# A two-block transformer layer on one core: padded parameter rows, the last expert behind the overflow tests, a final stage by halves, and down weights in 16 KB runs with a strided moving operand

## The reference

```python
(jax.nn.silu(xblk @ w1[e]) * (xblk @ w3[e])) @ w2[e]     # w1, w3: 1024 x 512, w2: 512 x 1024
```

## Time and profile before

| | |
|---|---|
| median of three runs (lowest, highest) | 1033.22 us (1032.62, 1033.77) |
| the profiled execution's own time | 1032.23 us |
| its span | 1030.4 us, 16914 instructions |
| PE busy (matmuls) | 96% of the span |
| PE weight loads busy | 74% |
| DVE, ACT, POOL busy | 38%, 37%, 12% |
| mean granted clock of TensorE | 0.988 of full |
| moved by DMA | 308 MB, 299 GB/s over the span |

### The profile page before, as it was taken

How to read it: one execution, slowest core, us unless ns; L and a number is a source line. 1 busy time by engine, 2 the same in 40 slices (tenths; PEclk the granted TensorE clock), 3 DMA queues, 4 the chain that set the end, 5 groups by cost and what they waited for, 6 DMA issues and landing times.

```text
span 1030.4 us, 16914 instructions
## 1 busy us (share of the span) xinstructions
PE 988.3 (96%) x7393; PEld 767.3 (74%) x7393; DVE 392.5 (38%) x750; ACT 377.1 (37%) x612; POOL 121.8 (12%) x81
## 2 busy tenths in 40 slices
PE   7999999999999999979999999989999999999996
PEld 6888789976555555545555555558989999999995
DVE  4446456853222111121222111127335444774475
ACT  4545646641111111111111111226445555554443
POOL 2110021020000000000000000002321111441122
PEclk8999999999999999998999999999999999999999
DMA  8974295788999999999999999997545544445301
GB/s 271 365 273 177 96 346 217 300 315 348 424 426 425 423 425 426 426 420 426 424 425 423 427 425 424 424 401 283 184 163 187 187 171 164 164 167 204 141 1 42
DMA packets 74829, 308.07 MB, mean 299 GB/s; under 512 B 5585, under 2 KB 12146, under 8 KB 58362
## 3 DMA queue, kind: packets, MB, share of 16 engines
q1 hardware_dynamic: 70962, 302.16, 74.0%
q10 hardware_dynamic: 3784, 4.73, 1.4%
HBM read 305.82 MB, written 2.63 MB: 299 GB/s over the span
## 4 chain that ended last, share of the span: by engine, by line
PE 85%; DVE 7%; ACT 4%; issue 2%; POOL 1%; DMA 1%; SPq 0%; ACTq 0%; DVEq 0%
PE bank L782 82%; DVE arena L1306 3%; DVE arena L1303 2%; PE bank L1251 1%; ACT arena L2058 1%; DVE wR L1300 1%; DMA arena<-in_rows 1%; PE bank L993 1%; DVE arena L1300 1%; ACT wR L1881 1%; POOL wR L2256 1%; ACT arena L2088 0%; DVE hTR L1300 0%; ACT arena L2086 0%; ACT arena L2111 0%
## 5 line engine op out<-in xcount | busy, mean ns | idle before, releaser
L782 PE MATMUL bank<-hTR,wR 128*128 128x256 f32 x2520 | 313.8, 284 | 4.2 <-DVE wR L1300 1.2
L782 PEld LDWEIGHTS bank<-hTR,wR 128*128 128x128 f32 x2520 | 305.1, 192 | 8.2 <-issue 4.2
L782 PE MATMUL bank<-ring,arena 128*64 128x256 f32 (+3 forms) x1680 | 229.6, 439 | 7.1 <-issue 7.1
L1300 DVE TENSOR_TENSOR wR<-ring,wR 128x1024 fp32r<-128x1024 f32 x126 | 157.8, 1259 | 133.2 <-ACT wR L1881 132.6
L1881 ACT ACTIVATE wR<-ring 128x1024 fp32r<-128x1024 f32 x161 | 168.5, 1055 | 109.2 <-PE bank L782 107.4
L782 PEld LDWEIGHTS bank<-ring,arena 128*64 128x64 f32 (+2 forms) x1680 | 115.3, 137 | 103.1 <-issue 59.7
L782 PE MATMUL bank<-arena 128*64 128x256 f32 (+7 forms) x1178 | 166.5, 406 | 0.7 <-DVE small L1432 0.7
L1306 DVE SCALAR_TENSOR_TENSOR arena<-bank,small,arena 128x256 f32<-128x256 f32 x32 | 15.5, 484 | 346.9 <-ACT arena L2058 346.9
L2029 ACT ACTIVATE arena<-bank,small 64x512 f32<-64x512 f32 x62 | 42.4, 684 | 280.5 <-PE bank L782 280.1
L782 PEld LDWEIGHTS bank<-arena 128*64 128x64 f32 (+3 forms) x1178 | 92.3, 144 | 62.4 <-issue 28.3
L2256 POOL TENSOR_TENSOR wR<-ring,wR 128x1024 fp32r<-128x1024 f32 x35 | 85.5, 2443 | 321.7 <-ACT wR L1881 321.7
(11 more groups left out here) (209 smaller groups left out, 823.2 us busy)
## 6 DMA issues: line engine op xcount, KB each, us to landing
ring<-in_w SPq DMA_DIRECT2D x39, 2048.0 KB, 21.5
ring<-in_w_in SPq DMA_DIRECT2D x29, 2048.0 KB, 8.4
arena<-in_w SPq DMA_DIRECT2D x25, 2048.0 KB, 19.0
ring<-in_w SPq DMA_DIRECT2D x42, 1024.0 KB, 19.4
arena<-in_w SPq DMA_DIRECT2D x22, 1024.0 KB, 20.9
ring<-in_w_ada SPq DMA_DIRECT2D x6, 2048.0 KB, 7.9
ring<-in_w_o SPq DMA_DIRECT2D x2, 2048.0 KB, 12.4
ring<-in_w_o_attn SPq DMA_DIRECT2D x2, 2048.0 KB, 7.9
```

The lines of the kernel that those rows point to most:

```text
L782: return pe.e.matmul(o, l, r, start=start, stop=stop)
L1300: return eng.tensor_tensor(o, a, b, op)
```

## The change

It does nine things.

1. The rows table is padded on the host with zeros from 113 to 128 rows, and all 128 are loaded.
2. The identity's DMA moves from SP's queue, where it was the first, to ACT's, ahead of ACT's first wait.
3. PE runs three warm-up matmuls behind the rows' transpose instead of five.
4. The transposes `turn1` and `turn3` get PSUM banks 2 to 5, one each, instead of banks 0, 1, 6 and 0 again.
5. A down weight is loaded by one DMA of 2 MB with four rows, 16 KB, a partition.
6. So that the hidden columns fit these rows, half `h` of an up product takes of every four columns of its weights the two from 2 `h` on. The moving operand becomes 128 pairs with a gap of two elements behind each.
7. ACT and DVE make the overflow test ahead of the last expert, which stands whole in both branches.
8. The gating of `wx0` stands between the splits of `wx1`, `n` = 0 ahead of the last split and `n` = 1 behind it.
9. At the end each row tile is gated, summed and scaled before the next: `final(n)` follows DVE's work on `n`, and ACT scales tile 0 ahead of the squares of tile 1.

```diff
         def expert_chunk(e, tag, what):
 
             if what == "d":
-                w2 = t["w2"][0, e].rearrange("(g p c) n -> p g c n", g=2, c=2)
-                return (tag, what, e), (w2[:, 0], w2[:, 1])
+                return (tag, what, e), (t["w2"][0, e].rearrange("(p k) n -> p k n", k=4),)
...
-            PB.use(("hT1", j2), PR.next())
+            PB.use(("hT1", j2), 2 + j2)
...
-            PB.use(("hT3", j2), PR.next())
+            PB.use(("hT3", j2), 2 + j2)
...
-        last4 = list(O2.chunk("wx1", uses, "m"))
+        last4 = O2.chunk("wx1", uses, "m")
+        first = next(last4)
+        O2.add("gate_rows", 0, 0)
+        last4 = [first] + list(last4)
+        O2.add("gate_rows", 0, 1)
         O2.add("evict", "wx0", None)
         for st in last4[:2]:
             O2.add(*st)
         O2.add("last_rows", last4[2][1], last4[3][1], uses)
-        O2.add("evict", "wx1", None)
+        for n in range(NT):
+            O2.add("gate_rows", 1, n)
+            O2.add("last_squares", n)
...
-            eng.dma_start(ident[:, :], t["k_ident"]).then_inc(s_ident, 16)
             for n in range(NT):
                 eng.dma_start(XN[:, n, :], x_d[128 * n:128 * n + 128, :]).then_inc(s_x[n], 16)
-            eng.dma_start(VR[0:NROW, :], t["rows"]).then_inc(s_rows, 16)
+            eng.dma_start(VR[:, :], t["rows"]).then_inc(s_rows, 16)
...
-            warm(pe, banks[6], 5)
+            warm(pe, banks[6], 3)
...
-                    w13 = space((tag, "ab"[m], e)).rearrange("p (k n) -> p k n", k=8)
+                    w13 = space((tag, "ab"[m], e)).rearrange("p (k q c) -> p k q c", k=8, c=4)
                     for j in range(8):
                         if e == 0 and m == 0 and j == 4:
                             for j_ in range(4, 8):
                                 gather(0, j_)
                         emptied(pe, P.of["g", r, b, j])
                         for h in range(2):
-                            last = mm(pe, bank[64 * h:64 * h + 64, 256 * m:256 * m + 256],
-                                      xe[b % 2][j // 4][:, j % 4, SLOTS * k:SLOTS * k + SLOTS], w13[:, j, 256 * h:256 * h + 256],
+                            last = mm(pe, bank[64 * h:64 * h + 64, 256 * m:256 * m + 256].rearrange("p (q c) -> p q c", c=2),
+                                      xe[b % 2][j // 4][:, j % 4, SLOTS * k:SLOTS * k + SLOTS], w13[:, j, :, 2 * h:2 * h + 2],
                                       j == 0, j == 7)
...
+                if lo == 0:
+                    for j in range(4):
+                        gathered(0, j)
+                    if not r:
+                        weights()
+                for e in range(lo, hi):
...
+                elif what == "gate_rows":
+                    c, n = a
+                    cs, u = slice(512 * c, 512 * c + 512), U_[f"wx{c}", n]
+                    filled(v, u)
+                    if c:
+                        v.wait_ge(s_gx[n], 1)
+                    tt(GT[n], banks[u.bank][:, :], grow[:, cs], ALU.mult).then_inc(u.free, 1)
+                    emptied(v, u)
+                    v.wait_ge(s_x2done[n], 1)
+                    tt(XN[:, n, cs], GT[n], XN[:, n, cs], ALU.add).then_inc(s_gx[n], 1)
+                    if c:
+                        v.wait_ge(s_gx[n], 2)
+                        v.wait_ge(s_fg, 16)
+                        v.step(tt(XO[:, n, cs], XN[:, n, cs], fg[:, cs], ALU.mult))
+                        final(n)
...
+            S = {n: sem(n) for n in MOE_SEMS}
+            experts(0, PB, S, 0, NE - 1)
             v.wait_ge(s_flag, 1)
             known = dict(v.known)
             with eng.If(eng.value_load(flag[0:1, 0:1]) > SLOTS):
-                last_low()
+                experts(0, PB, S, NE - 1)()
...
+                elif what == "last_squares":
+                    n = a[0]
+                    squares(1, n)
+                    if n == 0:
+                        s.wait_ge(s_rs[0], 4)
+                        s.wait_ge(s_fo[0], 1)
+                        eng.activation(XO[:, 0, :], XO[:, 0, :], ACT.Copy, scale=st3[:, 6:7]).then_inc(s_out[0], 2)
...
+            eng.dma_start(ident[:, :], t["k_ident"]).then_inc(s_ident, 16)
...
-    arrays["rows"] = np.concatenate([arrays.pop(n).reshape(-1, 128) for n in _ROWS])
+    rows = np.concatenate([arrays.pop(n).reshape(-1, 128) for n in _ROWS])
+    arrays["rows"] = np.concatenate([rows, np.zeros((128 - len(rows), 128), rows.dtype)])
```

More of the change, by code:

```diff
@@ L1609, in experts @@
                     select(0)
-                for j in range(4):
-                    gathered(0, j)
-                if not r:
-                    weights()
-                for e in range(NE):
+                if lo == 0:
[4 more added lines that the diff above has]
+                for e in range(lo, hi):
                     b, k = divmod(e, EB)
@@ L1725, in second_steps @@
                            ALU.mult).then_inc(u.free, 1)
-                    elif nm in ("wx0", "wx1"):
-                        c = int(nm[2])
-                        cs = slice(512 * c, 512 * c + 512)
-                        for n in range(NT):
-                            u = U_[nm, n]
-                            filled(v, u)
-                            if c:
-                                v.wait_ge(s_gx[n], 1)
-                            tt(GT[n], banks[u.bank][:, :], grow[:, cs], ALU.mult).then_inc(u.free, 1)
-                            emptied(v, u)
-                            v.wait_ge(s_x2done[n], 1)
-                            tt(XN[:, n, cs], GT[n], XN[:, n, cs], ALU.add).then_inc(s_gx[n], 1)
-                            if c:
-                                v.wait_ge(s_gx[n], 2)
-                                v.wait_ge(s_fg, 16)
-                                v.step(tt(XO[:, n, cs], XN[:, n, cs], fg[:, cs], ALU.mult))
+                elif what == "gate_rows":
[13 more added lines that the diff above has]
+                        final(n)
                 elif what == "norm2":
@@ L1802, in second_steps, with final @@
                     split_into(flat2(mRh, 2 * jj), flat2(mRl, 2 * jj), T[0], s_mh, jj + 1, s_m)
-            def final():
-                for n in range(NT):
-                    b, w = st3[:, 4 + n:5 + n], st3[:, 6 + n:7 + n]
-                    v.wait_ge(s_sq3[n], 2)
-                    v.step(tt(b, st3[:, 2 * n:2 * n + 1], st3[:, 2 * n + 1:2 * n + 2], ALU.add))
-                    v.settle()
-                    ts(b, b, 1.0 / D, EPS, ALU.mult, ALU.add).then_inc(s_var[n], 1)
-                    if n == 1:
-                        v.wait_ge(s_rs[1], 4)
-                        v.wait_ge(s_fo[1], 1)
-                        ts(XO[:, 1, 0:512], XO[:, 1, 0:512], w, None, ALU.mult).then_inc(s_out[1], 1)
+            def final(n):
+                b, w = st3[:, 4 + n:5 + n], st3[:, 6 + n:7 + n]
+                v.wait_ge(s_sq3[n], 2)
+                v.step(tt(b, st3[:, 2 * n:2 * n + 1], st3[:, 2 * n + 1:2 * n + 2], ALU.add))
+                v.settle()
+                ts(b, b, 1.0 / D, EPS, ALU.mult, ALU.add).then_inc(s_var[n], 1)
+                if n == 1:
+                    v.wait_ge(s_rs[1], 4)
+                    v.wait_ge(s_fo[1], 1)
+                    ts(XO[:, 1, 0:512], XO[:, 1, 0:512], w, None, ALU.mult).then_inc(s_out[1], 1)
             v.wait_ge(s_x[1], 16)
@@ L1826, in vector_program @@
             route()
-            last_low = experts(0, PB, dict(zip(MOE_SEMS, [sem(n) for n in MOE_SEMS])))
+            S = {n: sem(n) for n in MOE_SEMS}
+            experts(0, PB, S, 0, NE - 1)
             v.wait_ge(s_flag, 1)
@@ L1851, in vector_program @@
                     second_steps(*step)
-            final()
         def scalar_program(eng):
@@ L2018, in route, with experts @@
                 eng.activation(ex5, ex5, ACT.Exp).then_inc(s_rexp, 1)
[L2020 removed]
+            def experts(r, P, S, lo=0, hi=NE):
                 g = max(r - 1, 0)
@@ L2090, in second_norm, with squares @@
                 eng.activation(XV[:, 0, :], XS2[:, 0, :], ACT.Copy, scale=tw[:, 10:11]).then_inc(s_norm[0], 1)
+            def squares(c, n):
+                s.wait_ge(s_gx[n], c + 1)
+                if c:
+                    s.wait_ge(s_sq3[n], 1)
+                eng.activation(JK[n], XN[:, n, 512 * c:512 * c + 512], ACT.Square,
+                               accum_out=st3[:, 2 * n + c:2 * n + c + 1]).then_inc(s_sq3[n], 1)
             def bias(h):
@@ L2210, in scalar_program @@
             route()
-            finish = experts(0, PB, dict(zip(MOE_SEMS, [sem(n) for n in MOE_SEMS])))
+            S = {n: sem(n) for n in MOE_SEMS}
+            experts(0, PB, S, 0, NE - 1)
             s.wait_ge(s_flag, 1)
@@ L2214, in scalar_program @@
             with eng.If(eng.value_load(flag[0:1, 0:1]) > SLOTS):
-                finish()
+                experts(0, PB, S, NE - 1)()
                 s.wait_ge(s_scat, NE // 2)
```

15 lines of the change are left out of this document (3 added, 12 removed).

## The result

| | before | changed |
|---|---|---|
| median of five runs each (lowest, highest) | 1033.03 us (1031.97, 1033.77) | 1038.21 us (1037.27, 1039.90) |
| the profiled execution: own time, span | 1032.23, 1030.4 us | 1038.31, 1036.5 us |

The change made the kernel slower: 5.2 us, ratio 1.0048, 95% interval 1.0035 to 1.006. The forecast was 1027.2, range 1024.5 to 1032.5, faster; it started from 1033.2, the median of the first three runs.

A forecast was written before the change was run, and what follows sets the result against it. PE was taken as the bound, busy 988.3 of 1030.4 us. Gains of 3.3 (start), 0.2 (banks), 0 (experts), 1.3 (test) and 1.2 (end) sum to 6.0, so 1033.2 becomes 1027.2 us; range 1024.5 to 1032.5.

The forecast's parts named there:

- Experts: strided moving operand: Experts' up products, 1024 slots of 0.235 us: reading two elements and skipping two was taken to cost nothing.
- The dear ends: Experts' up products: upper prices from L1251's strided weight load, 67 us charged by the jump, 134 us by the column.
- The stride costs: Rival, experts' 1024 slots: skipping elements costs, deciding from 6 ns a slot; 1094 us by jump, 1161 by column; chance 0.15.
- the mild stride: Experts' up products: the strided operand costs a few ns, total 1028 to 1036 us; chance 0.08.
- the up products' mean above 395 ns: Sign of being wrong, in the experts: mean time an instruction above 395 ns, against 383 and 386 before.
- The start (3.3 us): Start: padded rows and first weights land earlier, fewer warm-ups; ACT evicts at 9.95 instead of 13.26, 3.3 us gained.
- Banks (0.2): First block: transposes' own PSUM banks free the first product from waiting for DVE; 0.2 us, between 0 and 1.0.
- Down weights (0): Experts: one 2 MB DMA replaces two of 1 MB, hidden behind PE with 0.8 us in hand at expert 30; nothing gained.
- Overflow test (1.3): Behind the last expert: ACT's test moves one expert earlier into idle time, so 1.3 us go (0.8 to 1.5).
- End (1.2): Final stage by halves: one power, no 1.15 us scaling ahead of the last; 1.2 us gained (0.4 to 1.5).
- the table not being the bound: Rival, start: first weights still land near 12.2 us, start gives 1.8 instead of 3.5; 1028.9 us, chance 0.10.
- the weights becoming it: Rival, last experts: each down weight 0.1 us dearer to load, last 3.2 us late, 0.8 covered; 1029.6 us, chance 0.05.

The follow-up runs named there:

- both undone: Changed kernel with the up products' moving operand contiguous again and each down weight in two 1 MB DMAs again: 1026.20 us, ratio to before 0.9930.
- the new DMA and a contiguous operand: Changed kernel with its 2 MB down-weight DMAs kept but a contiguous moving operand, so another product is computed: 1026.69 us, ratio to before 0.9937.
- the start alone: Kernel before plus only padded rows, identity on ACT's queue, three warm-ups and own banks for the first block's transposes: 1031.18 us, ratio 0.9989.
- the rest alone: Kernel before plus only the moved overflow test, final stage by halves, gating between splits and second block's banks: 1030.70 us, ratio 0.9979.

## Why the prediction was wrong

**The step that failed: "Experts: strided moving operand ... I take nothing".** It is 10.7 ns a slot, 11 us of busy PE, 11.7 to 12.0 us in the two comparisons. The dear ends (65 and 131 ns a slot) were as wrong as the zero. The argument went: one stream was seen to pass over 512 elements in 0.235 us, so passing over 512 and using 256 asks for no more than has been seen. That takes the rate of the slot from what is passed over. But the rows it leaned on were fp32r products, and their 512 elements are 128 lines with four used floats each; a line was never left after two. The runs show the cost to hang on how many floats of a line are used, 0 at four, 4.5% at two, 100% at one, and none of the rows that the zero rested on had a moving operand with fewer than four. The row that had fewer, the strided weight load, 207 against 142 ns, spoke for a cost and has two hits a line as well. It was set aside as another kind of operand, though it was the only one with the property in question. It stayed at 207 ns after the change.

**The rivals.** "The stride costs" had the right place and the right point of decision (6 ns a slot, and 10.7 is beyond it) but a price of 67 or 134 us; the mild stride, "a few ns, 1028 to 1036", came nearest, and 10.7 ns lies beyond it. The truth lay in the gap between them: by the forecast's own terms 1027.2 + 11.0 = 1038.2, which is the measured median. That it fits to the tenth is in part luck, since the start gave less than its term and the end more. Chances were given to two prices and none to what lay between. The sign of being wrong, "the up products' mean above 395 ns", was set too high as well: the means came to 395 and 391, and it was not crossed by a kernel that is slower by 5.2 us. A mean rose by 8 to 9 ns where a slot rose by 10.7, so the break-even of 6 ns a slot would have stood at some 388 and 391.

**The start (3.3 us).** Mechanism right for the DMAs: the padded table lands in 5.0 us, and the weights behind it early. Size 2.2 at 61 us in the changed kernel, 2.7 with both undone, 2.8 with the new DMA and a contiguous operand, 2.4 in the start alone. "The identity's issue ... costs nothing", as "warm-ups ... are over long before the rows now", was wrong: on ACT's queue, beside x and no longer ahead of it, it took 4.5 us to land. The nine warm-ups started at 5.28 in place of 2.73 and took 4.2, and the rows' transpose at 9.29 waited for them, not for the rows (1.64 + 5.0 = 6.6). The step left out when the identity itself would land. Of the 1.3 us by which ACT evicted later than forecast (11.25, 9.95) this is 0.9: DVE's scaling followed the rows' copy at 9.91, while POOL's power had ended at 8.98. The other 0.45 is x, "everything from x on 0.45 earlier": it was issued that much earlier, but ACT's first squares on it began at 5.05 (4.92 before) and POOL's power ended as before (8.97). With both undone they began at 4.45, so this part differs between executions. What the change of PE's pace gave (0.23 to 0.14 us a matmul, above) stood in no term. **Banks (0.2):** not measured apart. The first 24 products took 3.33 us, and the next began 3.5 us behind them (14.35, 17.84), after a wait of 0.16 us for DVE's split. That it is DVE's split that they wait for was foreseen.

**Down weights (0)** and **turn3's banks (0):** right; the form of the DMA alone made no difference, and the offset stayed at +7.5 us from the second block's transposes (704.41 before) to 832.83.

**Overflow test (1.3):** 1.31 in the changed kernel, 1.30 in the rest alone, with ACT's eviction 0.04 us behind PE. Right also in that the new place had cover. **End (1.2):** 1.5 in each of them, the upper end.

**The sum.** The forecast was 1027.2 with a free stride; the kernel without the stride took 1026.2. By place its gains are 2.75 at the start, 1.3 at the test and 1.5 at the end, 5.6 us, close to the 5.7 by which its profiled execution is faster (1026.55 against 1032.23). The medians differ by 6.8; the 1.2 us more are of the size of one clock episode, and no trace of one execution can say more of them. (The ends of the forecast's terms add up to 1025.9, not 1026.0; nothing hangs on it.)

The rival of the table not being the bound and that of the weights becoming it both fell: the first weights landed near 2.1 + 8.7 = 10.8 us, ACT's first split followed its eviction without a wait, and PE never waited for a weight DMA in the experts.

## What to carry to other kernels

Count, for a strided moving operand of a matmul, how many elements it uses of each 16-byte line of SBUF. In the plain float32 products here, two column tiles at a time, four were free with the gaps tried (4 and 128), two cost 4.5% of the product, one doubled it, and runs shifted off their lines cost 22%. So put a stride in blocks of four floats, aligned, or on the other side of the transfer; here the 16 KB run it was meant to buy was worth nothing, since PE and not the weights was the bound. And when a DMA is moved to another queue "for free", ask what waits for it first: here it was the warm-ups, and through them 0.9 us of the start.

## What the runs showed that was not expected

- Two used floats a line are at the edge and cost 4.5%, independent of DMA load (10.7 ns a slot at 426 GB/s, 10.6 at 152) and nearly so of the length of a product (9.7 ns with 128 columns). One is a full factor of two.
- Pairs in one tile and a contiguous operand in the other cost more (14.0 ns a slot) than pairs in both (10.7).
- The identity, 64 KB, issued at the same moment as x on another queue (0.74 and 0.72 us), landed in 4.5 us; issued first on x's queue at 0.72, as before, it let the warm-ups start at 2.73.
- TensorE's granted clock fell to half behind short holes in some executions and not in others. At 74 to 80 us this lasted 2 to 4 us and cost 1.5 us each time. At 230 to 240 us it lasted up to 8 us, and the same work took 25.19 us in the changed kernel with the clock at 1.00, 26.48 in the kernel before and 27.82 in the rest alone: at least 1.3 and 2.6 us. That is as much as any of the change's small parts.
- The same overflow test left ACT idle for 5.36 us in one program and 6.30 in another that differs from it only in the first microseconds.
